# Routing an MoE layer by ranks, with the overflow rows worked out later and filler matmuls before the first expert

## The reference

```
def hierarchical_moe(h, wc, bc, wf, bf, w_gate_up, w_down):
    ...
    coarse_prob = jax.nn.softmax((xt @ wc + bc).astype(jnp.float32), axis=-1)
    g_prob, g_idx = lax.top_k(coarse_prob, 1)
    fine_logits = (xt @ wf + bf).astype(jnp.float32).reshape(n, N_GROUPS, EXPERTS_PER_GROUP)
    fine_sel = jnp.take_along_axis(fine_logits, g_idx[:, :, None], axis=1)[:, 0]
    e_logit, e_idx = lax.top_k(fine_sel, TOP_K_INNER)
    e_w = jax.nn.softmax(e_logit, axis=-1) * g_prob
    ...
    gu = jnp.einsum('nd,edf->nef', xt, w_gate_up)
    gate, up = jnp.split(gu, 2, axis=-1)
    act = jax.nn.silu(gate) * up * gates.astype(h.dtype)[..., None]
    return jnp.einsum('nef,efd->nd', act, w_down).reshape(b, t, d)
```

## Time and profile before

| | |
|---|---|
| median of three executions | 1273.44 us |
| the profiled execution | 1275.61 us, of which the span is 1273.5 us |
| TensorE (PE) matmuls | 1137.3 us busy, 89% of the span |
| vector engine (DVE) | 663.3 us, 52% |
| scalar engine (ACT) | 592.0 us, 46% |
| POOL | 416.0 us, 33% |
| DMA | 194.86 MB, mean 153 GB/s |
| mean granted TensorE clock | 0.939 of full speed |

### The profile page before, as it was taken

One profiled execution on the slowest core, in us unless ns is written; L12 is line 12 of the kernel. 1 busy time (PEld: TensorE's weight loads), 2 busy tenths in 40 slices (PEclk: granted clock), 3 DMA queues, 4 the chain that ended last, 5 costly groups with the idle time before them and its releaser, 6 DMA issues.

```text
span 1273.5 us, 19313 instructions
## 1 busy us (share of the span) xinstructions
PE 1137.3 (89%) x6971; PEld 914.7 (72%) x6971; DVE 663.3 (52%) x908; ACT 592.0 (46%) x843; POOL 416.0 (33%) x350
## 2 busy tenths in 40 slices
PE   6998999999997499995699999999989993999990
PEld 5786888788786388784588668886668883788770
DVE  4334334388635599994606122430221335899984
ACT  5555243232424288985233332233322242789871
POOL 4332212110132233445254225442233251334432
PEclk9989999999798699998699999999989995999995
DMA  8331311112036669995443223332122166599955
GB/s 250 69 81 34 68 36 49 37 37 99 17 92 240 208 230 367 368 371 184 178 124 93 66 74 98 86 106 62 62 83 83 50 224 241 165 363 360 373 188 207
DMA packets 89282, 194.86 MB, mean 153 GB/s; under 512 B 19901, under 2 KB 21241, under 8 KB 88186
## 3 DMA queue, kind: packets, MB, share of 16 engines
q1 hardware_dynamic: 67562, 160.00, 38.1%
q10 hardware_dynamic: 11856, 17.07, 3.8%
q0 software_dynamic: 9792, 16.80, 3.6%
HBM read 189.63 MB, written 23.07 MB: 167 GB/s over the span
## 4 chain that ended last, share of the span: by engine, by line
PE 79%; DVE 9%; ACT 5%; DMA 3%; issue 2%; POOL 1%; POOLq 0%; DVEq 0%; SPq 0%; ACTq 0%
PE ps L583 22%; PE ps L585 20%; PE ps L584 20%; PE ps L2211 3%; PE ps L2220 2%; PE ps L2021 2%; ACT wh L1143 1%; DMA hs<-arena 1%; PE ps L1877 1%; DMA arena<-hs,slot_rows 1%; DVE arena L1327 1%; DMA arena<-y 1%; PE ps L2194 1%; PE ps L1908 1%; PE ps L2203 1%
## 5 line engine op out<-in xcount | busy, mean ns | idle before, releaser
L743 POOL TENSOR_TENSOR wl<-raw,wh 128x1024 fp32r<-128x1024 f32 x100 | 241.5, 2423 | 487.7 <-ACT wh L909 487.4
L583 PE MATMUL ps<-wh,hT_hi 128*128 128x512 f32 x928 | 379.8, 409 | 17.9 <-DVE hT_lo L1375 8.1
L585 PE MATMUL ps<-wh,hT_lo 128*128 128x512 f32 x928 | 367.2, 396 | 0.0
L584 PE MATMUL ps<-wl,hT_hi 128*128 128x512 f32 x928 | 366.5, 395 | 0.0
L909 ACT ACTIVATE wh<-raw 128x1024 fp32r<-128x1024 f32 x116 | 122.0, 1059 | 251.4 <-PE ps L585 230.3
L583 PEld LDWEIGHTS ps<-wh,hT_hi 128*128 128x128 f32 x928 | 177.7, 191 | 62.9 <-issue 15.1
L585 PEld LDWEIGHTS ps<-wh,hT_lo 128*128 128x128 f32 x928 | 177.2, 191 | 39.1
L584 PEld LDWEIGHTS ps<-wl,hT_hi 128*128 128x128 f32 x928 | 177.9, 192 | 35.0 <-issue 1.0
L583 PE MATMUL ps<-hT_hi,wh 128*128 128x512 f32 x288 | 118.2, 410 | 7.3 <-ACT arena L1052 5.3
L1698 DVE TENSOR_TENSOR wl<-arena,wh 128x1024 fp32r<-128x1024 f32 x96 | 117.6, 1225 | 12.7 <-ACT wh L1143 4.7
L1698 DVE TENSOR_TENSOR wl<-raw,wh 128x1024 fp32r<-128x1024 f32 x92 | 112.2, 1225 | 18.0 <-ACT wh L909 9.8
(11 more groups left out here) (291 smaller groups left out, 1318.5 us busy)
## 6 DMA issues: line engine op xcount, KB each, us to landing
raw<-in_moe_w_gate_up_dram SPq DMA_DIRECT2D x64, 512.0 KB, 8.7
arena<-in_moe_w_gate_up_dram SPq DMA_DIRECT2D x64, 512.0 KB, 8.5
raw<-in_odd_w_in_dram SPq DMA_DIRECT2D x48, 512.0 KB, 3.7
raw<-in_even_w_in_dram SPq DMA_DIRECT2D x32, 512.0 KB, 4.6
arena<-in_moe_w_down_dram SPq DMA_DIRECT2D x32, 512.0 KB, 7.9
raw<-in_moe_w_down_dram SPq DMA_DIRECT2D x32, 512.0 KB, 9.6
arena<-y ACTq DMA_DIRECT2D x8, 1024.0 KB, 8.2
raw<-in_odd_w_out_dram SPq DMA_DIRECT2D x16, 512.0 KB, 3.5
```

The costliest lines, as they stand in the source:

```text
L583: nc.tensor.matmul(dst, lh, rh, start=first, stop=False)
L584: nc.tensor.matmul(dst, lh, rl, start=False, stop=False)
L585: return nc.tensor.matmul(dst, ll, rh, start=False, stop=last)
L743: pool.tensor_tensor(wl[:, i % NSPL, :, :], raw_at(i), wh[:, i % NSPL, :, :].bitcast(F32), ALU.subtract).then_inc(lo_pool, 1)
```

## The change

- The slots of the first 128 pairs of every expert are found straight from the one-hot rows and the ranks: `hotA` is `oh` times the pair's row number, made before the ranks are there, and `hotB` compares the rank with 0 to 127. A pair of rank 128 or more meets no column there. The overflow tiles have factors of their own (`hotO`, and `hotB` again), made on DVE in `overflow_slots` and `overflow_hot`, a second product on TensorE behind the first expert's gate_up, and `overflow_rows` on DVE behind the first expert's product. The pair weights follow there.
- `slots_to_rows` is the former product as a function, for 16 and for 7 tiles.
- The last hs tile is multiplied by the norm's weight on DVE right behind the copy of the last transposes, and scaled and stored by ACT in `outnorm`.
- The logits of tile T go to PSUM bank T % 2, and the first half of tile 3's goes ahead of tile 2's.
- SP waits for both first gathers ahead of piece m+12.
- The splits of m+2 and m+3 go behind `overflow_slots`.
- `warm(n)` issues n matmuls of 128 x 512 whose result nobody reads: 14 behind the slot product, 4 behind the first `xT`. The first half of the splits of xT is enough for the first two quarters of expert 0.
- The load of the next norm's weight goes behind the first SiLU on ACT's queue.

```diff
+        hotO = v3(bf(RO + 1812, 16 * (SLOT_TILES - NE)), 8)
-        rows_at = ps[:, 2, 0:2 * SLOT_TILES]
+        logits_at = ps[:, 0:2, 0:40].rearrange("p b (t c) -> p t b c", t=2)
+        rows_at, over_at = ps[:, 2, 0:2 * NE], ps[:, 7, P:P + 2 * (SLOT_TILES - NE)]
...
-                        sp.wait_ge(s_("r_logits"), l + 1)
-                        sp.wait_ge(s_("h_stored0"), 32 * (l + 1))
+                        for q in range(2):
+                            sp.wait_ge(s_(f"xg_loaded{q}"), 144 * l + 16)
...
-                    act.wait_ge(s_("h_ready"), 4 * n + T + 1)
+                    if T < NT - 1:
+                        act.wait_ge(s_("h_ready"), h_count(n, T))
...
+                act.wait_ge(s_("norm_w_applied"), 2 * l + 2)
+                act.wait_ge(s_("norm_r"), 4 * n + NT)
+                A(act.activation(hrow(NT - 1), hrow(NT - 1), ACT.Copy, scale=rs[:, NT - 1:NT]))
+                store(NT - 1)
...
-                act.wait_ge(s_("h_ready"), 4 * (2 * l + 1) + NT)
-                act.dma_start(hs_dram[l].rearrange("(T p) d -> T p d", p=P)[NT - 1], hrow(NT - 1)).then_inc(s_("h_stored1"), 16)
-                load_wb(2 * l + 2)
...
+                load_wb(2 * l + 2)
...
-                D(tt(rw, rw, nw.unsqueeze(2).broadcast_to([P, KD, 20]), ALU.mult), s_("rw_scaled"))
+                D(tt(rw, rw, nw.unsqueeze(2).broadcast_to([P, KD, 20]), ALU.mult), s_("norm_w_applied"))
...
                 D.read(dve.tensor_copy(hTf[:, 4:8, cols(NT - 1)], v3(tile(name), 4)), name)
+                D(tt(hrow(NT - 1), X[:, NT - 1, :], wb(2 * l + 1), ALU.mult), s_("norm_w_applied"))
 
...
-                D(tt(lg, v3(ps[:, 0, 0:80], 4), bc_h(rs, 20), ALU.mult))
+                by_bank = lg.rearrange("p (t b) c -> p t b c", b=2)
+                D(tt(by_bank, logits_at, rs.rearrange("p (t b) -> p t b", b=2).unsqueeze(3).broadcast_to([P, 2, 2, 20]), ALU.mult))
...
-                scaled(l, NT - 1)
+                for j in range(2):
+                    c, of_pair = slice(NE * j, NE * (j + 1)), tokv[:, 8 * j:8 * j + 8]
+                    D(tt(hotA[:, :, c], oh.rearrange("p T j e -> p (T j) e"), of_pair.unsqueeze(2).broadcast_to([P, 8, NE]), ALU.mult))
...
+                D(tt(sl8, oh, at.unsqueeze(2).broadcast_to([P, 4, 2, NE]), ALU.mult))
+                D(dve.tensor_reduce(slotf, sl8.rearrange("p T j e -> p (T j) e"), AX.X, ALU.add))
+                for n in (0, 4):
+                    D(tt(hotB[:, n:n + 4, :], iotaB.unsqueeze(1).broadcast_to([P, 4, P]),
+                         slotf[:, n:n + 4].unsqueeze(2).broadcast_to([P, 4, P]), ALU.is_equal), s_("r_hot"))
...
+                dve.wait_ge(s_("r_rows"), 2 * l + 1)
+                slot_rows(rows_at, slice(0, NE), s_("rows_known"))
+            def slot_rows(found, c, on):
+                D(dve.tensor_reduce(rowf[:, c], v3(found, 2).rearrange("p j n -> p n j"), AX.X, ALU.add))
+                D(dve.tensor_copy(idx[:, 1, c], rowf[:, c]))
+                D(ts(idx[:, 0, c], idx[:, 1, c], 1, None, ALU.logical_shift_right), on)
+            def overflow_slots(l):
+                at = v3(ps[:, 7, 0:64], 4)
...
+            def overflow_hot():
+                n7 = SLOT_TILES - NE
...
-                D(tt(hitA, iotaA.unsqueeze(1).broadcast_to([P, 8, SLOT_TILES]), slotA.unsqueeze(2).broadcast_to([P, 8, SLOT_TILES]), ALU.is_equal))
+                D(tt(hitA, iotaA[:, NE:SLOT_TILES].unsqueeze(1).broadcast_to([P, 8, n7]), slotA.unsqueeze(2).broadcast_to([P, 8, n7]), ALU.is_equal))
...
-                    c = slice(SLOT_TILES * j, SLOT_TILES * (j + 1))
-                    D(tt(hotA[:, :, c], hitA, tokv[:, 8 * j:8 * j + 8].unsqueeze(2).broadcast_to([P, 8, SLOT_TILES]), ALU.mult))
+                    D(tt(hotO[:, :, n7 * j:n7 * (j + 1)], hitA, tokv[:, 8 * j:8 * j + 8].unsqueeze(2).broadcast_to([P, 8, n7]), ALU.mult))
...
-                dve.wait_ge(s_("r_rows"), l + 1)
-                D(dve.tensor_reduce(rowf, v3(rows_at, 2).rearrange("p j n -> p n j"), AX.X, ALU.add))
-                D(dve.tensor_copy(idx[:, 1, :], rowf))
-                D(ts(idx[:, 0, :], idx[:, 1, :], 1, None, ALU.logical_shift_right), s_("rows_known"))
+            def overflow_rows(l):
+                dve.wait_ge(s_("r_rows"), 2 * l + 2)
+                slot_rows(over_at, slice(NE, SLOT_TILES), None)
...
+            def pair_weights(l):
...
 
+                overflow_slots(l)
                 lo_in(m + 2)
                 lo_in(m + 3)
+                overflow_hot()
                 xT_lo(l, 0, 0)
...
                 gated(16 * l, 0)
+                overflow_rows(l)
+                pair_weights(l)
 
...
-                def logits(T):
-                    for k in range(KD):
-                        if k == KD // 2:
+                def logits(T, halves_of_row=(0, 1)):
+                    for hf in halves_of_row:
+                        if hf == 1:
...
-                        ins = mm(ps[:, 0, 20 * T:20 * T + 20], hTf[:, k, cols(T)], rw[:, k, :], start=k == 0, stop=k == KD - 1)
-                    if T == NT - 1:
+                        for k in range(4 * hf, 4 * hf + 4):
+                            ins = mm(logits_at[:, T // 2, T % 2, :], hTf[:, k, cols(T)], rw[:, k, :], start=k == 0, stop=k == KD - 1)
+                    if T == NT - 1 and halves_of_row[-1] == 1:
...
                 tile_is_read(pe, ("xT", l, 0, NT - 1))
-                pe.wait_ge(s_("rw_scaled"), l + 1)
+                pe.wait_ge(s_("norm_w_applied"), 2 * l + 1)
                 logits(0)
...
                 finish(3, (3,))
+                logits(3, (0,))
                 logits(2)
                 rawT(l, 1, 3)
-                logits(3)
+                logits(3, (1,))
 
...
+            def warm(n):
+                for _ in range(n):
+                    mm(ps[:, 3, :], HTH[:, 7, 0:P], HTH[:, 6, :], start=True, stop=True)
+            def slots_to_rows(dst, token, nobody, hot):
+                mm(dst, ones_b, nobody, start=True, stop=False)
+                for n in range(8):
+                    if n % 4 == 0:
+                        pe.wait_ge(s_("r_hot"), hot + n // 4 + 1)
+                    ins = mm(dst, hotB[:, n, :], token[:, n, :], start=False, stop=n == 7)
+                return ins
...
-                mm(rows_at, ones_b, empty, start=True, stop=False)
-                for n in range(8):
-                    if n % 4 == 0:
-                        pe.wait_ge(s_("r_hot"), 2 * l + n // 4 + 1)
-                    ins = mm(rows_at, hotB[:, n, :], hotA[:, n, :], start=False, stop=n == 7)
-                ins.then_inc(s_("r_rows"), 1)
+                slots_to_rows(rows_at, hotA, empty, 4 * l).then_inc(s_("r_rows"), 1)
+                warm(14)
...
+                warm(4)
...
-                pe.wait_ge(s_("xT_lo"), 32 * l + 4)
+                pe.wait_ge(s_("xT_lo"), 32 * l + 3)
...
+                pe.wait_ge(s_("xT_lo"), 32 * l + 4)
...
+                pe.wait_ge(s_("r_hot"), 4 * l + 4)
+                slots_to_rows(over_at, hotO, empty[:, 2 * NE - SLOT_TILES:SLOT_TILES], 4 * l + 2).then_inc(s_("r_rows"), 1)
```

More of the change, by code:

```diff
@@ L119, in evac_count, with h_count @@
     return 4 * sum(evac_engine(b) == evac_engine(db) for b in range(db)) + t + 1
+def h_count(n, T):
+    return sum(NT - (m in (1, 3)) for m in range(n)) + T + 1
 def lo_by_dve(i):
@@ L627, in build @@
         first = reg(RO + 1576, NE)
-        hitA = v3(bf(RO + 1592, 8 * SLOT_TILES), 8)
-        hotA = v3(bf(RO + 1684, 16 * SLOT_TILES), 8)
+        hitA = v3(bf(RO + 1592, 8 * (SLOT_TILES - NE)), 8)
+        hotA = v3(bf(RO + 1684, 16 * NE), 8)
+        hotO = v3(bf(RO + 1812, 16 * (SLOT_TILES - NE)), 8)
         hotB = v3(bf(RO + 1868, 8 * P), 8)
-        empty = bf(RO + 2500, 2 * SLOT_TILES)
-        rows_at = ps[:, 2, 0:2 * SLOT_TILES]
+        empty = bf(RO + 2500, 2 * NE)
+        logits_at = ps[:, 0:2, 0:40].rearrange("p b (t c) -> p t b c", t=2)
+        rows_at, over_at = ps[:, 2, 0:2 * NE], ps[:, 7, P:P + 2 * (SLOT_TILES - NE)]
         rowf = reg(RO + 2530, SLOT_TILES)
@@ L727, in _ @@
             for T in range(NT):
-                sp.wait_ge(s_("h_ready"), 4 * 4 + T + 1)
+                sp.wait_ge(s_("h_ready"), h_count(4, T))
                 sp.dma_start(out[0].rearrange("(T p) d -> T p d", p=P)[T], htok(4)[:, T % 2, :]).then_inc(s_(f"out_stored{T % 2}"), 16)
@@ L1355, in outnorm @@
                 D(dve.memset(any80[:, 64:80], 0.0))
-                D(dve.memset(empty[:, 0:SLOT_TILES], EMPTY / P))
-                D(dve.memset(empty[:, SLOT_TILES:2 * SLOT_TILES], 0.0))
+                D(dve.memset(empty[:, 0:NE], EMPTY / P))
+                D(dve.memset(empty[:, NE:2 * NE], 0.0))
                 add(0)
@@ L1837, in norm @@
                         rows(MOE_AT[0], T - 2)
-                    pe.wait_ge(s_("h_ready"), 4 * n + T + 1)
+                    pe.wait_ge(s_("h_ready"), h_count(n, T))
                     for g in range(2):
```

## The result

The changed kernel took 1259.79 us (median of 4 executions, 1258.22 to 1261.06), the kernel before 1273.34 beside it (4 executions, 1272.63 to 1281.03). The ratio is 0.9882, with a 95% interval of 0.9859 to 0.9904. The two medians lie 13.6 us apart; by the ratio the change is 15.0 us faster, or 12.2 to 18.0. The forecast was 1256.5 in a range of 1253 to 1264; the time lies 3.3 above the one and inside the other, and just past the 1% line of 1260.7. The profiled execution took 1259.16 (span 1257.1) against 1275.61 (span 1273.5): 16.4 less, where the steps had summed to 17.0.

A forecast was written before the change was run, and what follows sets the result against it. TensorE matmuls were taken to bound nearly four fifths of the span, except on the way into each expert loop. Gains 7.5 + 1.75 and 5.5 + 2.3 sum to 17.0, giving 1256.5 us from 1273.44; range 1253 to 1264.

The forecast's parts named there:

- The estimate of 3.2: First gather: the skill page's fit gives 3.2 us for 0.52 MB, forecast 2.2 lower over both layers; prediction kept 4.3.
- the 3.9: Routing up to the indices: scaling, slot operations and a wait leave the chain, 3.9 us less than today's 13.10.
- indices + 7.65: DVE's queue from the indices to xT's half split: gate_up at 423.75 / 1073.15, 0.3 behind TensorE's own 423.45.
- The shift of 0.85: Logits: tile 3's first half, moved ahead of tile 2's, delays transposes, copy and second half by 0.85 us.
- The bound of 0.8 for the clock: Last eight logits matmuls: the clock might fall or hold differently; taken as zero, kept as 0.8 us either way.
- near 1079: Sign of being right: ACT at the m+6 split near 429 in the first layer and 1079 in the second.
- The first rival: Clock down again when gate_up starts: gate_up 1.3 later and 0.4 longer, 1.7 per layer, 1259.8 us; chance 0.22.
- the second: Rival: weight loads held until the second gather starve the expert loop, slower at 1292 us; chance 0.04.
- the third: Rival: later gathers or splits collide with late loads, or DVE's longer queue delays xT and aT; 1265 us, chance 0.12.
- the fourth: Rival: hs store no earlier because ACT waits for a late product; 1271 us, chance 0.04.
- Same work: From the first expert's split on: table load, SiLU, product and transposes unchanged, overflow's small matmuls fit TensorE's 2 us hole.
- the 2.85: Overflow rows and pair weights on DVE behind the first product: zero cost, at most 2.85 us without cover.

The follow-up runs named there:

- store_early: Kernel before with only the last hs tile multiplied on DVE behind the copy and scaled and stored early by ACT; 1270.65 us.
- slots_kept: Kernel before plus early store, SP's later wait, fillers and half wait for xT, without ranks, overflow's move and half logits; 1260.51 us.
- before_filler: Kernel before with only the 14 and 4 filler matmuls added; 1269.06 us.
- loads_early: Changed kernel with SP's old wait ahead of piece m+12, so weight loads run beside the last hs store and first gathers; 1262.68 us.
- overflow_gap: Changed kernel with the overflow product ahead of the first gate_up, its rows behind xT's first splits, pair weights at the loop's end; 1256.98 us.
- best_hole: best plus eight filler matmuls behind the first expert's gate_up, in the hole ahead of expert 1; 1252.67 us.
- logits_whole: Changed kernel with tile 3's logits in one piece again, behind their transposes; 1256.08 us.
- after_again: Changed kernel repeated word for word; 1258.14 us.
- hole_filler: Changed kernel with six more filler matmuls behind the first expert's gate_up, ahead of the first SiLU's wait; 1258.30 us.
- no_filler: Changed kernel without its 14 and 4 filler matmuls; 1264.53 us.
- best: Changed kernel with the edits of logits_whole, overflow_gap and clear_first together; 1255.73 us.
- clear_first: Changed kernel with the gather buffer cleared ahead of the wait for the router's constants instead of behind it; 1257.30 us.

## Why the prediction was right, and where it was not

**Store, indices, gather.** Right. The store left both chains, the indices came 9.19 after R (forecast 9.2), and the gather took 4.74 / 4.46, near the forecast 4.3. The estimate of 3.2 by the fit of the Trainium skill, "DMA: Bandwidth & Descriptors", Anatomy of one DMA, was not met. The parts of the 3.9 were sized wrong against each other: the scaling was worth 0.93, not 1.32 (store_early), ranks and shorter products 2.98, not 2.6 (slots_kept). From indices to gather took 0.30, not 0.95. That 0.9 had been read off a gather released by a DMA's landing; before_filler, also released by the store, shows 0.85 / 0.76 of issue there as well, while every kernel whose gather was released by DVE has 0.30. What in that hand-over takes the other half microsecond, no run separates.

**DVE's queue, not the gather, fixed gate_up.** The prediction had this too, "indices + 7.65": gate_up came at indices + 7.64 / 7.57, whether the gather took 4.3 or 4.7. DVE goes from the indices through the overflow's slots and hot pieces to the low split of xT without a pause (423.18), and TensorE, done with transposes and fillers, waits for that split. So the prediction was wrong where it said that a gather of 3.2 would make the forecast 2.2 lower: by its own sum DVE's queue ended last, and an earlier landing gained nothing. It also shows what is still to be had. In slots_kept, where less stands ahead of that split, X to E is 2.17, against 2.54 to 2.97 in the kernel after and its repetition; moving the hot pieces behind the split was not tried.

**Logits.** The shift of 0.85 came in both layers. The bound of 0.8 for the clock was reached in the second: eight matmuls at 1.91 instead of 1.08, 1.73 lost where 0.85 stood in the sum. Nearly all of what the second layer lacked up to S (6.85 gained, 7.8 forecast) is this term.

**xT to gate_up, clock.** X to E 2.55 / 2.78 against 2.35, for X came earlier behind the indices than forecast and E did not; E to S 5.36 / 5.35 against 5.2. ACT's split of m+6 came at 429.34 and 1070.96. The first is the forecast's 429. The second missed "near 1079" by 8 us, as the transposes missed "1070 to 1072" (1062.83): those sentences left out what the first layer had already gained, the sum did not (1086.14 - 9.25 - 7.8 = 1069.1). The clock was up at about 417.9, 1.7 us earlier than forecast. The first rival did not come in the kernel after. Its rule (the Trainium skill, "TensorE: Matmul & The Clock Gate", Part 4: a transpose doesn't count as busy) may hold: behind up to 2.39 us of idle time and eight transposes the clock stayed up in every kernel with filler but loads_early, where it fell in one of two passages behind 3.4. There gate_up ran 1.2 longer, not the 0.4 of the rival. The median of 1259.79 is the 1259.8 that this rival had named; that is chance, since its clock was not there.

**The other rivals.** No wait for a weight transfer stands on TensorE or ACT between 430 and 470, so the second is out. DVE's queue kept TensorE idle for 0.45 and 0.69 behind the four fillers, a shadow of the third, but one that the sum had in it. Of the fourth nothing came: ACT issued the store of tile 3 at 407.53, and it landed 2.6 later.

**"Same work" from the split on, and "Zero" for the 2.85.** Both failed, with opposite signs. The clock stayed up ahead of expert 1 and gave 1.6 a layer (overflow_gap and best_hole 40.6, against 42.2 with the clock down). DVE's queue took back 0.3 to 0.4 of it (kernel after 40.95). This net 1.2 a layer, 2.42 in all, was in no term of the sum, and with the clock lost in 7 of 18 such passages it is luck that both layers had it. When the clock falls there, the queue is covered: logits_whole 42.15, the same as before.

**Between the layers** 1.84 went, in no term either. In the kernel after the chain passes through the router's setup on DVE and TensorE waits for tile 0's sum (1031.63, then 1032.38). The kernel before shows 436.05, the variants 434.1 to 438.7 for changes that lie elsewhere. Behind the setup the chain goes back over the loads of its constants on ACT's queue, of which two issues took 4.07 and 2.19. The setup beside POOL's splits is part of it (below), but does not explain it: overflow_gap had the slow setup and 435.1, logits_whole the quick one and 436.5. What fixes its phase stays open.

So the way up to the first gate_up was right by its mechanism, but that the profiled total came within 0.6 us of the sum is luck, because three misses cancelled: forecast 17.05; less 1.14 up to the split, plus 2.42 in the hole, less 1.84 between the layers, gives 16.49 of the 16.4 seen. By the executions it is 13.6 between the medians and 15.0 by the ratio, or 16.2 between those of after_again.

Of the whole gain, the early store alone brings 4.0; SP's wait, the filler and the half wait 10.1 on top; ranks, overflow's move and half logits together 0.7 to 2.4, which is within the noise (by the stages 2.4 besides the clock). SP's wait taken away alone costs 2.9 to 4.5, the filler 4.7 to 6.4.

## What to carry to other kernels

Where TensorE idles for a known chain of small operations and then starts a burst, dummy matmuls that end before the burst's data land pay for the burst's first microseconds; here they were the largest part that could be had with two lines, and needed no other change. The idle time behind them should be short: behind the fillers up to 2.4 us never cost the clock here and 3.4 us did once in two, while ahead of expert 1 some 2 us did in 7 of 18 passages. Splitting a short product to fill a hole costs its length wherever the filled hole is not what the chain waits for: look at what stands between the moved part and the next release. Read the price of a hand-over from a row with the same kind of releaser. And add up the queue of every engine from the last release to the burst: here the gather looked last, and DVE's queue was.

## What the runs showed of the hardware

**The length of TensorE's hole of about 2 us did not tell whether the clock outlives it.** Ahead of expert 1 it stayed up in both layers in five kernels (after, after_again, overflow_gap, hole_filler, best_hole), fell in both in four (before, no_filler, store_early, slots_kept), and did one of each in five. best fell behind 2.07 us of idle time in the first layer and held behind 2.06 in the second; clear_first held behind 1.84 and fell behind 1.84. Of the kernels with fillers in the hole none fell, in four passages; since 11 of 18 held without them, that is too few to call it shown.

**A small DVE cast that begins beside a POOL subtract lasts until its end.** Timeline of POOL in the kernel after, then DVE's and POOL's in the kernel before:

```profile
1023.38 7.20 POOL L749 TENSOR_TENSOR wl<-raw,wh 128x1024 fp32r<-128x1024 f32 x3 [6.33 <-ACT wh L915]
```

```profile
1037.11 0.23 DVE L1351 CAST arena<-arena 128x128 bf16<-128x128 f32 x1
```

```profile
1037.38 2.40 POOL L743 TENSOR_TENSOR wl<-raw,wh 128x1024 fp32r<-128x1024 f32 x1 [0.49 <-ACT wh L909]
```

The cast took 0.23 in POOL's gap and 2.30 beside its third subtract: it ended at 1030.67, 0.1 behind POOL's 1030.58. In the 28 setups of the fourteen kernels it began inside a subtract eleven times and took 2.29 to 2.43 each time, and 0.23 the other seventeen. The 128x160 product before it took 1.17 and 1.72, both beside a subtract, and 0.33 without one (after_again, first layer). The Trainium skill, "SBUF — State Buffer", "Who interferes with whom", describes such an exclusive lock of a shared port pair; the trace agrees. Together they made the second layer's setup 2.6 longer than in the kernel before, as much as several of the edits weighed here; how much of it reached TensorE is open, as said above.
